# A hybrid transformer kernel: two expert matrices loaded earlier, and the order of work inside two attentions changed

## The reference

```
h     = rmsnorm(x) * (1 + sc1) + sh1            # latent stream (256 tokens) and context stream (256)
a     = attention of 6 heads, keys of 64 + 32:  # 64 from a low-rank projection, 32 rotary, shared by all heads
        softmax(qn kn^T + qr kr^T) v            # latent queries see context and latent keys
b     = attention of 6 heads of 64, banded mask, with a sink term in the softmax
x     = x + g1 * (concat(a, b, short_conv) @ w_o)
aff   = softmax((rmsnorm(x) * (1 + sc2) + sh2) @ router_w)   # over 16 experts
idx   = top-k tokens for each expert            # 32 of the 256 tokens, per stream
x     = x + g2 * sum_e top_aff * (silu(xg @ w_gate[e]) * (xg @ w_up[e])) @ w_down[e]
```

## Time and profile before

| | us |
|---|---|
| median of three runs | 2215.16 |
| profiled execution, whole | 2216.35 |
| its span | 2214.4 |
| PE busy | 2055.4 (93%) |
| DVE busy | 917.6 (41%) |
| ACT busy | 448.1 (20%) |
| mean DMA rate | 197 GB/s |

### The profile page before, as it was taken

One profiled execution on the slowest core, in us unless ns is written; L12 is line 12 of the kernel. 1 busy time (PEld: TensorE's weight loads), 2 busy tenths in 40 slices (PEclk: granted clock), 3 DMA queues, 4 the chain that ended last, 5 costly groups with the idle time before them and its releaser, 6 DMA issues.

```text
span 2214.4 us, 32671 instructions
## 1 busy us (share of the span) xinstructions
PE 2055.4 (93%) x14117; PEld 1595.4 (72%) x14117; DVE 917.6 (41%) x1884; ACT 448.1 (20%) x985; POOL 86.3 (4%) x87
## 2 busy tenths in 40 slices
PE   6999999999899888667999999999999998999998
PEld 2444586555565476546878878899987788889998
DVE  2137723233326632214445523466414544146662
ACT  3004512111122421001323112100003411220001
POOL 1000010000000000000001100000000011000000
PEclk9999999999999999778999999999999999999999
DMA  9750518999923379997432224446543321244462
GB/s 370 253 201 27 204 49 339 411 424 426 407 79 110 122 286 415 425 424 283 149 106 91 76 77 152 152 153 178 147 154 113 114 86 60 97 147 166 151 168 81
DMA packets 182145, 435.70 MB, mean 197 GB/s; under 512 B 6346, under 2 KB 72818, under 8 KB 166130
## 3 DMA queue, kind: packets, MB, share of 16 engines
q1 hardware_dynamic: 180864, 431.19, 52.7%
q10 hardware_dynamic: 1138, 2.41, 0.3%
HBM read 432.53 MB, written 1.05 MB: 196 GB/s over the span
## 4 chain that ended last, share of the span: by engine, by line
PE 83%; DMA 10%; DVE 4%; ACT 2%; issue 1%; ACTq 0%; DVEq 0%
PE bank L284 78%; DMA ring<-in_exp_w_up 4%; DMA ring<-in_exp_w_gate 2%; PE bank L617 1%; PE bank L886 1%; DMA ring<-in_exp_w_down 1%; DMA ring<-in_w_in 1%; DMA cst<-in_exp_w_up 1%; DMA arena<-in_x 1%; DVE arena L835 0%; ACT h L740 0%; ACT arena L840 0%; DVE arena L940 0%; PE bank L1517 0%; PE bank L538 0%
## 5 line engine op out<-in xcount | busy, mean ns | idle before, releaser
L284 PE MATMUL bank<-h,ring 128*128 128x256 f32 (+2 forms) x3360 | 738.7, 378 | 16.4 <-ACT arena L671 5.1
L284 PEld LDWEIGHTS bank<-h,ring 128*128 128x128 f32 x3360 | 591.5, 191 | 145.8 <-issue 66.5
L284 PE MATMUL bank<-arena 128*128 128x128 f32 (+11 forms) x3528 | 459.1, 328 | 42.5 <-issue 9.7
L284 PEld LDWEIGHTS bank<-arena 128*128 128x128 f32 (+5 forms) x3528 | 344.8, 171 | 133.5 <-issue 63.9
L284 PE MATMUL bank<-arena,ring 128*128 128x128 f32 (+1 forms) x1704 | 267.9, 317 | 1.0 <-PE bank L284 1.0
L284 PEld LDWEIGHTS bank<-arena,ring 128*128 128x128 f32 x1704 | 245.9, 191 | 19.6 <-PE bank L284 1.8
L840 ACT ACTIVATE arena<-bank 128x256 f32<-128x256 f32 (+4 forms) x227 | 100.5, 461 | 523.0 <-PE bank L284 493.7
L835 DVE COPY arena<-bank 128x512 f32<-128x512 f32 (+6 forms) x90 | 50.7, 565 | 237.3 <-PE bank L284 160.6
L284 PE MATMUL bank<-ring,arena 128*32 128x128 f32 (+1 forms) x1600 | 122.4, 356 | 26.4 <-DMA ring<-in_exp_w_up 13.7
L284 PEld LDWEIGHTS bank<-ring,arena 128*32 128x32 f32 (+1 forms) x1600 | 85.0, 135 | 66.0 <-DMA ring<-in_exp_w_up 17.8
L284 PE MATMUL bank<-h,arena 128*128 128x128 f32 (+2 forms) x640 | 103.4, 320 | 2.6 <-ACT arena L1508 2.6
(11 more groups left out here) (365 smaller groups left out, 1664.6 us busy)
## 6 DMA issues: line engine op xcount, KB each, us to landing
ring<-in_w_in SPq DMA_DIRECT2D x32, 2048.0 KB, 8.0
ring<-in_exp_w_up SPq DMA_DIRECT2D x21, 2048.0 KB, 14.9
ring<-in_ada_w SPq DMA_DIRECT2D x18, 2048.0 KB, 10.2
ring<-in_exp_w_gate SPq DMA_DIRECT2D x16, 2048.0 KB, 13.4
ring<-in_exp_w_down SPq DMA_DIRECT2D x16, 2048.0 KB, 16.0
ring<-in_w_ffn_gate SPq DMA_DIRECT2D x10, 2048.0 KB, 7.8
ring<-in_w_ffn_up SPq DMA_DIRECT2D x10, 2048.0 KB, 7.8
arena<-in_exp_w_down SPq DMA_DIRECT2D x9, 2048.0 KB, 17.7
```

The source lines that it names most:

```text
L284: return PE.matmul(o, lhsT, rhs, start=(k == 0), stop=(k == n - 1))
```

## The change

- The load order of layer 0's end: expert 0's down matrix and expert 1's gate matrix go in front of the last two modulation chunks.
- DVE's rounds in the attentions of both layers: normalise first, then the copy, then the modulation step.
- In the step before the attention, the four dummy matmuls go, and ACT's six copies of the rotary rows stand before its evictions of keys and values.
- The weighting of the selections: for the first stream at n = 8 (expert 4) in both layers, for the second stream, which only layer 0 has, at n = 12 as before.
- Ten dummy matmuls in place of six in layer 1's routing.

```diff
         load_order = list(range(len(stream)))
+        experts_at = last_expert[0] - 3 * NE + 1
+        early = [experts_at + 2, experts_at + 3]
+        load_order[experts_at - 2:experts_at + 4] = early + [experts_at + i for i in (-2, -1, 0, 1)]
         first = last_expert[L - 1] - 3 * NE + 1
...
                 if i < len(heads):
                     stats(i)
+                if 1 <= i <= len(heads):
+                    normalise(i - 1)
+                if i >= 2:
+                    out_turned(i - 2, 1)
                 if between and i <= len(heads):
                     between(i)
-                if i >= 2:
-                    out_turned(i - 2, 1)
-                if 1 <= i <= len(heads):
-                    normalise(i - 1)
...
-            keep_busy(pe, 2)
             join(tensor, pe, ("heads", l))
...
+            act.wait_ge(*vector.at("rot", l, "kr"))
+            for i in range(H1):
+                SC.activation(k96[HI, i, :], krb[HI, 0, :], ACT.Copy).then_inc(*scalar.mark("chain"))
             for i in range(1, H1, 2):
                 out_scalar(act, k96[LO, i, :], bank("k96", l, i)[LO, :], "k96", l, i)
             for j in range(1, 4, 2):
                 out_scalar(act, vall[:, j, 0:384], bank("v_mla", l, j)[:, 0:384], "v_mla", l, j)
-            act.wait_ge(*vector.at("rot", l, "kr"))
-            for i in range(H1):
-                SC.activation(k96[HI, i, :], krb[HI, 0, :], ACT.Copy).then_inc(*scalar.mark("chain"))
...
-        GATHER_AT, AHEAD, WEIGHTED_AT = ((3, 12), (2, 6)), (8, 4), 12
+        GATHER_AT, AHEAD, WEIGHTED_AT = ((3, 12), (2, 6)), (8, 4), ((8, 12), (8,))
...
-            if n == WEIGHTED_AT:
-                dve.wait_ge(*tensor.at("xg", l, NS - 1, KD - 1, 1))
-                for s in range(NS):
+            for s in range(NS):
+                if n == WEIGHTED_AT[l][s]:
+                    dve.wait_ge(*tensor.at("xg", l, s, KD - 1, 1))
                     for j in range(2):
                         V.tensor_tensor(sel[l][s][j], ...
...
-                keep_busy(pe, 3)
+                keep_busy(pe, 5)
```

## The result

The changed kernel takes **2205.03 us** (median of 4 runs, 2203.02 to 2207.25) where the kernel before took 2216.2 us in the same session (2214.86 to 2219.17). The two medians differ by 11.2 us (ratio 0.9950); the ratio on record is 0.9936 with a 95% interval of 0.992 to 0.9952, which holds both. The forecast was 2203, range 2197 to 2211. The profiled execution has a span of 2202.3 us (before: 2214.4) and a mean granted clock of 0.981 (before: 0.975).

A forecast was written before the change was run, and what follows sets the result against it. PE is nearly always busy, so only its waits, half-speed stretches and DMA-paced stretches were taken to move the end. The terms summed to -12.6 us, 2203.7 for the profiled execution, 2202.6 for the median, rounded 2203; range 2197 to 2211.

The forecast's parts named there:

- join, layer 0, with the clock behind it: Before layer 0's attention: PE resumes at 188.9 instead of 192.12, -3.2 us; first scores at full speed, -1.8 us.
- join, layer 1: Before layer 1's attention: PE resumes at 709.2 instead of 712.43, -3.2 us.
- order, layer 0: Layer 0's attention: waits for normalise go, values wait for the copy in odd rounds; sum +0.5 us.
- order, layer 1, with its clock: Layer 1's attention: waits in round 8 and the last rounds go, -2.2 us; low clock over 752 to 759 goes, -3.1.
- a new fall: In the attentions: one of the new waits brings the clock down, +2.5 us, bounds 0 and 6.
- dummies: Layer 1's routing: ten dummies end 0.9 us ahead of their release, the low clock goes, -2.1 us.
- early loads, weighting: Layer 0's load order and both expert stages: buffer slots limit later loads, PE's gains are waited for later; 0 each.
- Rival D: At both joins: a DVE eviction ends as late as the copies did, joins don't move; 2211 us, 4 in 100.
- Rival C: Attentions' odd rounds: DVE has no slack, each values step waits a full normalise, 1.2 us; 2222 us, 5 in 100.
- Rival A: In the attentions: no clock gains, and the new waits bring two falls, +5 us; 2212 us, 12 in 100.
- Clock 1.00 to the end of the gathers: Sign for layer 1's routing: with the longer dummies the granted clock stays full until the gathers end.
- rival B: Layer 0's expert stage: the early matrices pay, the queue keeps its lead, another -7.8 us; 2195 us, 10 in 100.

The follow-up runs named there:

- run 6: The kernel before with only ACT's copies of the rotary keys moved ahead, the four filling groups before the join kept: 2208.52 us, one run.
- run 8: The changed kernel with DVE's copy ahead of normalise in odd attention rounds, normalise first in even ones: 2194.72 us, ratio 0.9898 to the kernel before.
- run 7: The changed kernel with half of the gate and up loads of layer 0's experts 10 and 11 left out: 2193.08 us, ratio 0.9887 to the kernel before.

## Why the prediction was right

By stretches, the forecast's terms beside the runs:

| term | forecast | measured |
|---|---|---|
| join, layer 0, with the clock behind it | -3.2 - 1.8 | -3.23 - 1.7 (value matmuls to first turn) |
| join, layer 1 | -3.2 | -3.24 (P1) |
| order, layer 0 | +0.5 | +0.26 (A0) |
| order, layer 1, with its clock | -2.2 - 3.1 | -5.1 (A1, means of six each, new falls in it) |
| a new fall | +2.5 | in the row above already, see below |
| dummies | -2.1 | -1.5 (R), -1.1 in the changed kernel |
| early loads, weighting | 0 | 0 (ratios 0.9998 and 0.9998) |

- **Joins.** Right in mechanism and size: the value eviction is what arrives last, PE's wait is 0.63 us, and the clock behind the join in layer 0 is full. Rival D is out. That the shorter wait matters more than the dummies is shown by run 6: same dummies, no wait, no fall. The eight traces without the 2.14 us of wait have no fall in layer 0's first scores, with the dummies or without, and the six with it all have one. The rule of the Trainium skill (page "TensorE: Matmul & The Clock Gate", section "What's actually happening"), by which the throttled state is the default and activity releases it, did not count against taking these four dummies out: in the seven traces without them the scores of both layers run at full speed.
- **Order.** The forecast priced 1.7 us for round 3, 1.2 and about 2.1 for rounds 9 and 11 of layer 1. The trace has 1.65, 1.07 and 2.10. The other odd rounds have less than 0.3, but for round 11 of layer 0, where it is 1.23 us, 0.67 more than before for the 0.5 forecast. In A1 PE's waits sum to 5.09 us where they were 6.93: -1.84 for the forecast's -2.2, whose own items add up to -2.1. Rival C needed VectorE to be late in all of them. What the forecast missed is that one fixed order is not the best one; run 8 gains 5.8 us by order alone.
- **The clock behind the new waits.** The forecast expected one of them to bring it down, +2.5. It does so in some executions: of the six traces with the change's order, A1 has no fall in three (49.7), 1.65 us in two and 3.26 in one, +1.1 in the mean, and A0 has one of 1.6 us only in the two with the old join. So the mechanism was right, and the term was about 1.4 us too dear. The old fall was priced too low: A1 is 5.47 us shorter in the changed kernel's profile, and less the 1.84 us of waits that leaves 3.6 for the clock, where 3.1 was forecast. Rival A, two falls and no gain of the clock, is what the order alone showed in its profile (low over 207 to 211 us, and still low in A1); the changed kernel did not.
- **Dummies.** The wait went from 2.79 to 1.06 us, near the 0.9 worked out, but the fall went in two of six traces only. "Clock 1.00 to the end of the gathers" was wrong for the changed kernel: 0.66 over 802 to 807.
- **Early matrices.** Worth nothing, as forecast, and rival B is out. The forecast's signs all came: an empty queue before expert 2's down matrix (0.06 over 380 to 385), the issue at the same distance behind the output projection (108.34 us; before 108.18), a landing after 7.7 us, stalls of 8.0 us against 7.8. The Trainium skill (page "DMA: Bandwidth & Descriptors", section "Rules for kernel authors") says to issue a DMA early and wait for it late, and the prediction read it as a rule by which the stalls would go. They did not: they lie at 478 to 583 us in the changed kernel, in a full queue whose loads are issued as buffers come free, 200 us and more behind the issue at 276, and run 7 shows that fewer bytes there do what an earlier issue elsewhere doesn't.
- **Weighting.** Right: 1.2 us less wait for VectorE, 1.2 more for DMA.

The measured terms sum to -4.93 - 3.24 + 0.26 - 5.1 - 1.5 = -14.5 us, 1.9 more than the forecast. The whole is known less well: the medians differ by 11.2 us, the ratios on record are 0.9936 (-14.2 of 2216.2) and 0.9923 (-17.1 of 2219.68), and the two profiles by 12.1. By stretches the 12.1 are S -5.53, A0 +0.26, M +0.18, P1 -2.03, A1 -5.47, R -1.09 and T +1.58. So the total comes as near to -12.6 as it does partly by luck: the 2.5 us set aside for a new fall in the attentions were not spent there in this trace, and the dummies gave 1.0 us less than forecast, while P1 met a low clock over 615 to 622 us that takes 1.2 us more than in the other traces with the new join, and T came out 1.6 us longer, which no part of the change explains. What is not settled is why the clock falls in one execution of the same code and not in the next; the two traces of the changed kernel show that it does, and nothing here tells what decides.

## What to carry to other kernels

Find what arrives last at a join and ask whether an idle engine could have done it earlier; here six copies behind the last evictions cost 3.2 us twice, and more by the clock. An order for an in-order engine is to be chosen round by round: if the consumer alternates between two needs, the producer's order may have to alternate too (-5.8 us over the one fixed order here). Ask of a load that is to be issued earlier whether issue time is what holds the late ones; here buffers released them into a full queue, an earlier issue elsewhere gave nothing, and fewer bytes there gave 8 us. And for changes of a few us, cut the traces at milestones close around each change: such stretches repeat within 0.3 us where totals scatter by several, and long ones (S, T) scatter by up to 4 us themselves.

## What the runs showed of the hardware

- A wait of PE of 2.14 us ahead of the first scores was followed by a low granted clock in layer 0 in six of six traces; in layer 1, behind the same wait, it was so with the new order (two of two) and in one of four with the old one. A length of wait alone does not decide it.
- The cost of a fall comes in steps where PE sets the pace: stretches are about 1.7 us longer for each, in P1 (106.81 and 108.51), A0 (82.17 and 83.80) and A1 (49.69 and 51.35). Where DMA sets it, in layer 0's expert stage, a fall behind the 2.4 us wait cost 0.2 us or less (M 329.46 and 329.62 with it, 329.45 to 329.53 without any).
- With filling matmuls that end 1.06 us before the next work the clock stayed up in two of six traces; with six groups, which left 0.20 us, it did in the one trace there is.
- Four megabytes taken out of a full queue gave 8.0 us; at the 425 GB/s of the earlier trace rows their transfer takes 9.9 us.
